# Spans of a gated linear attention: four short-format products on halves of the log decays in place of two f32 products

## The chip, the cores and the metric

The kernel runs on one core of one Trainium2 chip. The metric is the device time in microseconds (us) of one execution. A core has TensorE (PE, matrix products into PSUM), VectorE (DVE), ScalarE (ACT), GpSimd (POOL) and a queue for DMAs (SP). Each engine works through its own queue in order; between engines there are semaphores.

## The reference

One decoder layer on 1024 tokens of width 1024: a half-step SwiGLU network, a mixing layer of three head groups, a second half-step SwiGLU network. The change is in the mixing layer. Its linear-attention group takes this from the input projection:

```python
def gla(q, k, v, out_gate, gate_lr, w_gate_up, b_gate, norm_gain):
    log_a = jax.nn.log_sigmoid((gate_lr @ w_gate_up + b_gate).astype(jnp.float32)) / GLA_TAU
    ...
    b = jnp.cumsum(chunked(log_a, GLA_DK), axis=3)
    diff = b[..., :, None, :] - b[..., None, :, :]
    decay = jnp.exp(jnp.where(causal[:, :, None], diff, -jnp.inf))
    A = jnp.sum(qc[..., :, None, :] * kc[..., None, :, :] * decay, axis=-1)
    o_intra = jnp.einsum('bhnij,bhnjd->bhnid', A, vc)
    ...
    o_inter = jnp.einsum('bhncd,bhnde->bhnce', qc * jnp.exp(b), s_prev)
```

The sums of `log_a` over stretches of tokens are what the kernel calls spans. The other two groups are a sliding-window attention (window 128, 8 heads, with sinks and a relative bias) and an attention over 256 memory tokens (4 heads).

## The kernel before

The mix goes over the 1024 tokens in NB = 8 blocks of 128. The order on each engine is written out by hand, and semaphores with counts tie the engines together. I call one turn of the loop a pass; pass n does the work of block n and prepares block n + 1.

PE in pass n (`mix_tensor`): `mem_scores(n)` (L1809), `levels(n)` (L1841, 56 records), `turn(0, n)` (L1856, transposes of the probabilities of head group 0), `scores(0, n+1)` (L1753), `spans_of(n+1)` (L1763), `turn(1, n)` (L1856), the turned keys (L1863), `gla_out(n)` (L1879, L1882), `scores(1, n+1)`, `key_values(n)`, `turn(2, n)`, `values(0, n)` and `values(1, n)` (L1893), `mem_values(n)` (L1908). In pass 0 the memory scores and the levels stand slightly otherwise: the spans of block 0 and the scores of block 0 are made between the last products of the input projection, and `turn(0, 0)` is ahead of `levels(0)`.

`spans_of` multiplies the log decays of one block, `log_a[:, n, :]` (128x128, f32), by a constant matrix `spans` of zeros and ones (128x1024), in two products of 512 columns, into PSUM banks 2 and 3. An f32 product leaves two records in the trace. Products in the short format (F32R) leave one, and the kernel takes an f32 product elsewhere by splitting an operand in a high and a low half of that format (`split_product`, L57 to L59).

Three waits matter. `turn(1, n)` waits for `level_taken` at 7(n + 1): seven predicated copies on DVE (`take_levels`, L2088) which fetch the levels from the banks that the turn overwrites. `scores(0, n+1)` waits for the exponentials of memory attention of the same pass on ACT (`mem_exps`, L1986), which read the same banks. `spans_of(n+1)` waits for ACT's copy of the turned probabilities (`pt_copy(0, n)`, L2004), banks 2 and 3 again.

ACT in pass n (`mix_scalar`): the rest of `exps(1, n)` (L1969, L1974), `mem_exps(n)`, `pt_copy(0, n)`, `gate_decays(n+1)` (L1955 to L1962, the exponentials of the spans), `k_hat_copy` (L2009), `pt_copy(1, n)`, `o_copy`, `exps(0, n+1)`, `pt_copy(2, n)` (L1999), `swa_hi` (L2026), the first head of `exps(1, n+1)`, `mem_hi(n)` (L2031). In passes 4 and 5 a square (L1393) comes in before `mem_hi`.

DVE in pass n (`mix_vector`): `gate_edges` (L1793), `denominators(1, n)` (L1799, L1802), `take_levels(n)`, `mem_denominators(n)` (L2074; in pass 0 it is ahead of the copies), the row maxima of block n + 1 (L1773 to L1786), `gate_q` (L1823), `denominators(0, n+1)`, `swa_lo` (L2109), `mem_lo` (L2114), `mem_max(n+1)` (L1817). POOL scales the probabilities (L2172), four instructions for each head group, and makes two products (L2156, L2163).

SBUF places are given by address. The 4 KB from 84 KB on belong to `hT_lo[:, 5, :]`, which the input projection reads to its last product; that product signals `proj_ready` at NG.

Of the kernel before, what the change touches and what calls it, by code (L numbers as in the profile page):

```python
# [9 lines left out]
F32 = mybir.dt.float32  # L10
# [51 lines left out]
def build(nc, x_in, mem_in, w_gate1, w_up1, w_down1, w_proj, w_mem, w_out, w_gate2, w_up2, w_down2, gains_in,  # L62
# [3 lines left out]
    with ctx:  # L66
# [28 lines left out]
        def place(at, *tensors):  # L95

            skip = [(f"skip{next(places)}", [P, at // 4], F32)] if at else []
            return phase(*skip, *tensors)[len(skip):]
# [18 lines left out]
        for f, order in enumerate((PARTS, PARTS[4::-1] + PARTS[5:])):  # L117
# [36 lines left out]
        p_hi, p_lo = place(120 * KB, ("p_hi", [P, 3, D], F32R), ("p_lo", [P, 3, D], F32R))  # L154
        w_rank = place(176 * KB, ("w_rank", [P, KT, RANK_ROWS], F32))[0]
        p_raw = place(184 * KB, ("p_raw", [P, 3, D], F32))[0]
        (PT1, spans, Pg1, A_T0, A_T1, decays, edges, k_hat_tok, state, span_end, chunk_decay, row_max, shift, sink_shift,
         sink_exp, row_sum, row_inv) = place(
            120 * KB,
            ("PT1", [P, 2, HALF], F32), ("spans", [P, SPLITS + 1, P], F32), ("Pg1", [P, 4, 2 * P], F32),  # L160
            ("A_T0", [P, GLA_HEADS, P], F32), ("A_T1", [P, GLA_HEADS, P], F32),
            ("decays", [P, SPLITS + 2, P], F32), ("edges", [P, 2, 2, P], F32), ("k_hat_tok", [P, P], F32),
            ("state", [P, GLA_DV], F32), ("span_end", [P, NB], F32), ("chunk_decay", [P, NB], F32),
            ("row_max", [P, 8], F32), ("shift", [P, 12], F32), ("sink_shift", [P, 8], F32),
            ("sink_exp", [P, 8], F32), ("row_sum", [P, 12], F32), ("row_inv", [P, 12], F32))
        A_T = (A_T0, A_T1)
        square_hi = place(180 * KB, ("square_hi", [P, 2, HALF], F32R))[0]
        square_lo = place(196 * KB, ("square_lo", [P, 2, HALF], F32R))[0]
        bias, Pg0 = place(184 * KB, ("bias", [P, SWA_HEADS, 2 * P], F32), ("Pg0", [P, 4, 2 * P], F32))
# [1587 lines left out]
        def spans_of(pe, n):  # L1757
            wait(pe, pt_ready, pt_count(0, n - 1))
            if n == 0:
                pe.wait_ge(spans_landed, 16)  # L1760
                pe.wait_ge(gate_summed, 2)
            for c in range(2):
                mm = nc.tensor.matmul(ps[:, SPAN_BANK + c, :], log_a[:, n, :], spans[:, 4 * c:4 * c + 4, :],  # L1763
                                      start=True, stop=True)
            mm.then_inc(span_summed, 1)

        def bias_max(dve, u, n, heads=range(4)):
            dve.wait_ge(scored, unit_count(u, n))
# [20 lines left out]
        def gate_edges(dve, n):  # L1789
            dve.wait_ge(decay_ready, 4 * n + 4)  # L1790
            wait(dve, o_ready, n - 1)
            wait(dve, k_hat_turned, n - 1)
            nc.vector.tensor_tensor(edges[:, n % 2, :, :], decays[:, SPLITS:SPLITS + 2, :], gqk[:, :, blk(n)], ALU.mult  # L1793
                                    ).then_inc(edge_ready, 1)
# [152 lines left out]
        def mix_scalar(act):  # L1947
# [17 lines left out]
            def exps(u, n, heads=range(4)):  # L1965
                act.wait_ge(shifted, SHIFTS * n + 2 * u + 1)
                for i in heads:
                    p, c = P_of[u][:, i, band(n)], 4 * u + i
                    nc.scalar.activation(p, p, ACT.Exp, bias=shift[:, c:c + 1], accum_out=row_sum[:, c:c + 1]  # L1969
                                         ).then_inc(probs_ready, 1)  # L1970
                if 3 not in heads:
                    return
                act.wait_ge(shifted, SHIFTS * n + 2 * u + 2)
                nc.scalar.activation(sink_exp[:, 4 * u:4 * u + 4], sink_shift[:, 4 * u:4 * u + 4], ACT.Exp  # L1974
                                     ).then_inc(probs_ready, 1)
# [53 lines left out]
            def mem_hi(n):  # L2029
                act.wait_ge(values_done, values_count(2, n))  # L2030
                nc.scalar.activation(hT_hi[:, 6:8, blk(n)], ps[:, O_BANK, 2 * P:4 * P].rearrange("p (j t) -> p j t", j=2),  # L2031
                                     ACT.Copy).then_inc(mem_y_hi_ready, 1)
# [2 lines left out]
            nc.scalar.activation(rstd_tok[:, 0:1], eps[:], ACT.Exp)  # L2035
            gate_decays(0)
            exps(0, 0)
            for n in range(NB):
                more = n + 1 < NB
                exps(1, n, range(begun(n), 4))  # L2040
                mem_exps(n)
                if not more:
                    out_gate(n)
                pt_copy(0, n)
                if more:
                    gate_decays(n + 1)
                    k_hat_copy(n)
                else:
                    for c in range(2):
                        head_root(act, GLA_OUT + c, HALF)  # L2050
                pt_copy(1, n)
                if not more:
                    unit_scalar(act, NPROJ)
                o_copy(n)
                if more:
                    exps(0, n + 1)
                    if n:
                        out_gate(n)
                pt_copy(2, n)
                if n == 0:  # L2060
                    out_gate(n)
                swa_hi(n)
                if n in FIRST_SQUARE_AT:
                    first_square(FIRST_SQUARE_AT.index(n))
                if more:
                    exps(1, n + 1, range(begun(n + 1)))
                mem_hi(n)

        def mix_vector(dve):

# [41 lines left out]
            def mem_lo(n):  # L2112
                dve.wait_ge(mem_y_hi_ready, n + 1)
                nc.vector.tensor_tensor(hT_lo[:, 6:8, blk(n)],  # L2114
                                        ps[:, O_BANK, 2 * P:4 * P].rearrange("p (j t) -> p j t", j=2),
                                        hT_hi[:, 6:8, blk(n)].bitcast(F32), ALU.subtract).then_inc(mem_y_lo_ready, 1)

            for n in range(NB):
                more = n + 1 < NB
                if n:  # L2120
                    gate_edges(dve, n)
                if not more:
                    gate_out(n - 1)
                denominators(dve, 1, n)
                if n == 0:
                    mem_denominators(n)
                take_levels(n)
                if more:
                    if n:
                        mem_denominators(n)  # L2130
                    bias_max(dve, 0, n + 1)
                    bias_max(dve, 1, n + 1, (0, 1))
                    update_state(n)
                    sink_difference(dve, 0)
                    bias_max(dve, 1, n + 1, (2, 3))
                    sink_difference(dve, 1)
                    gate_q(dve, n + 1)
                    if n:
                        gate_out(n - 1)
                else:  # L2140
                    gate_out(n)
                    head_invert(dve, GLA_OUT, HALF)
                    unit_vector(dve, NPROJ)
                    gla_apply(dve, 0)
                if more:
                    denominators(dve, 0, n + 1)
                swa_lo(n)
                mem_lo(n)
                if more:
                    mem_max(dve, n + 1)  # L2150

# [210 lines left out]
        def _(sp):  # L2362
# [19 lines left out]
            skewed = bias_dram.rearrange("(h x) -> h x", h=SWA_HEADS)[:, P - 1:P - 1 + P * (ROW - 1)]  # L2382
            sp.dma_start(bias[:], skewed.rearrange("h (p u) -> p h u", u=ROW - 1)[:, :, 0:2 * P]).then_inc(bias_landed, 16)
            sp.wait_ge(proj_ready, last_group[PROJ.index("mq1")])
            sp.dma_start(spans[:], spans_dram).then_inc(spans_landed, 16)
            sp.wait_ge(biased, 8 * NB)
            unit_sync(sp, NPROJ)
            sp.wait_ge(turned, unit_count(0, NB - 1))
# [269 lines left out]
```

## Time and profile before

| what | value |
|---|---|
| device time, median of 3 runs | 1685.02 us (1684.78 to 1685.14) |
| device time of the profiled execution | 1685.07 us |
| its span | 1683.3 us |
| busy PE, DVE, ACT, POOL | 99%, 66%, 43%, 33% |
| spans product in the chain of work that ended last | 1% of the span |
| mixing passes 0 to 7 | about 840 to 950 us from the start |

The page's first part has the busy time of each engine. Its fourth follows the work that ended last back from the end. The timeline lists instructions with start and duration in us; in square brackets stands the idle time of that engine before the instruction and who ended it. Neighbouring instructions of one kind are merged in it (x7 is seven); a narrow slice shows single ones.

### The profile page before, as it was taken

To read this page: it belongs to the slowest core of one execution; us is meant where nothing else is said; L and a number is where in the kernel's file an instruction comes from. 1 tells how busy PE (TensorE), PEld (TensorE's weight loads), DVE (VectorE), ACT (ScalarE), POOL (GpSimd) and SP (SyncE) were. 2 spreads that over 40 slices of the span, in tenths; PEclk is the share of its full clock that TensorE was granted. 3 is DMA by queue.
4 is the path that set the end of the run, shared out by engine and by line. 5 is a ranking of instruction groups with operands and counts; after the bars stand their busy time and mean duration, and the time that the engine had idled before them with its cause. 6 is when DMAs were issued, how large, how long until landed. Compare 5 with 4: busy or idle time off the path is not lost.

```text
span 1683.3 us, 25076 instructions
## 1 busy us (share of the span) xinstructions
PE 1673.6 (99%) x8399; PEld 1373.2 (82%) x8399; DVE 1115.0 (66%) x1581; ACT 726.9 (43%) x1378; POOL 552.0 (33%) x457
## 2 busy tenths in 40 slices
PE   9999999999999999999999999999999999999999
PEld 7888888888888889888767787888888888888887
DVE  7965555555489588458888935985555555569664
ACT  6533333333344465333378723443333333334442
POOL 0544445544130135012266422354444444310000
PEclk9999999999999999999999999999999999999999
DMA  7342222233774532120100223123333222584434
GB/s 215 81 144 94 100 100 93 100 106 117 263 258 144 163 94 88 63 84 17 38 2 2 64 75 138 38 107 107 119 113 110 93 93 106 185 285 149 144 99 165
DMA packets 101790, 191.73 MB, mean 114 GB/s; under 512 B 11539, under 2 KB 14068, under 8 KB 101708
## 3 DMA queue, kind: packets, MB, share of 16 engines
q1 hardware_dynamic: 100624, 188.50, 32.9%
q0 software_dynamic: 848, 2.10, 1.0%
q8 instruction: 48, 0.79, 0.2%
q14 instruction: 34, 0.28, 0.0%
q10 hardware_dynamic: 236, 0.06, 0.0%
HBM read 139.76 MB, written 50.86 MB: 113 GB/s over the span
## 4 chain that ended last, share of the span: by engine, by line
PE 96%; ACT 1%; DVE 1%; DMA 1%; issue 0%; SPq 0%; ACTq 0%; DVEq 0%
PE ps L57 30%; PE ps L59 30%; PE ps L58 30%; PE ps L1856 1%; PE ps L1763 1%; PE ps L1893 1%; PE ps L1753 1%; PE ps L1841 1%; DMA xT<-in_x 1%; ACT Pg L1969 0%; PE ps L1908 0%; DVE A_T L2088 0%; PE ps L1809 0%; PE ps L1879 0%; ACT glu L2004 0%
## 5 line engine op out<-in xcount | busy, mean ns | idle before, releaser
L521 DVE TENSOR_TENSOR ring<-w_raw,ring 128x512 fp32r<-128x512 f32 x240 | 239.9, 1015 | 219.4 <-ACT ring L516 219.2
L57 PE MATMUL ps<-hiT,ring 128*128 128x512 f32 x672 | 261.6, 389 | 0.0
L59 PE MATMUL ps<-hiT,ring 128*128 128x512 f32 x672 | 261.5, 389 | 0.0
L58 PE MATMUL ps<-loT,ring 128*128 128x512 f32 x640 | 249.0, 389 | 0.0
L57 PE MATMUL ps<-down_ring 128*128 128x512 f32 x616 | 239.7, 389 | 0.0
L59 PE MATMUL ps<-down_ring 128*128 128x512 f32 x616 | 239.7, 389 | 0.0
L58 PE MATMUL ps<-down_ring 128*128 128x512 f32 x616 | 239.7, 389 | 0.0
L57 PE MATMUL ps<-hiB,ring 128*128 128x512 f32 x576 | 224.8, 390 | 0.3 <-DVE loB L386 0.3
L59 PE MATMUL ps<-hiB,ring 128*128 128x512 f32 x576 | 224.2, 389 | 0.0
L516 ACT ACTIVATE ring<-w_raw 128x512 fp32r<-128x512 f32 x240 | 150.5, 628 | 169.9 <-PE ps L59 163.4
L895 ACT ACTIVATE down_ring<-down_raw 128x512 fp32r<-128x512 f32 x176 | 108.9, 629 | 222.9 <-DMA down_raw<-act_dram 176.1
L899 DVE TENSOR_TENSOR down_ring<-down_raw,down_ring 128x512 fp32r<-128x512 f32 x176 | 128.2, 737 | 110.8 <-ACT down_ring L895 110.5
L537 POOL TENSOR_TENSOR w_raw<-w_raw 128x512 f32<-128x512 f32 x40 | 58.3, 1462 | 298.0 <-DVE ring L521 281.5
L58 PE MATMUL ps<-loB,ring 128*128 128x512 f32 x384 | 149.4, 389 | 0.0
L57 PEld LDWEIGHTS ps<-hiT,ring 128*128 128x128 f32 x672 | 126.2, 188 | 26.5 <-issue 0.3
L59 PEld LDWEIGHTS ps<-hiT,ring 128*128 128x128 f32 x672 | 126.2, 188 | 26.3
L58 PEld LDWEIGHTS ps<-loT,ring 128*128 128x128 f32 x640 | 120.1, 188 | 24.8
L58 PEld LDWEIGHTS ps<-down_ring 128*128 128x128 f32 x616 | 115.6, 188 | 24.2
L57 PEld LDWEIGHTS ps<-down_ring 128*128 128x128 f32 x616 | 115.7, 188 | 23.9
L59 PEld LDWEIGHTS ps<-down_ring 128*128 128x128 f32 x616 | 115.6, 188 | 23.9
L57 PEld LDWEIGHTS ps<-hiB,ring 128*128 128x128 f32 x576 | 108.1, 188 | 23.2 <-issue 0.9
L59 PEld LDWEIGHTS ps<-hiB,ring 128*128 128x128 f32 x576 | 108.1, 188 | 22.6
(296 smaller groups left out, 3004.8 us busy)
## 6 DMA issues: line engine op xcount, KB each, us to landing
down_raw<-act_dram SPq DMA_DIRECT2D x154, 256.0 KB, 2.6
w_raw<-in_w_gate SPq DMA_DIRECT2D x88, 256.0 KB, 3.1
w_raw<-in_w_up SPq DMA_DIRECT2D x88, 256.0 KB, 3.2
act_dram<-actT SPq DMA_DIRECT2D x88, 256.0 KB, 2.0
act_dram<-act SPq DMA_DIRECT2D x66, 256.0 KB, 2.0
wd<-in_w_down SPq DMA_DIRECT2D x44, 256.0 KB, 4.8
wd_mirrored<-in_w_down SPq DMA_DIRECT2D x33, 256.0 KB, 4.4
p_raw<-in_w_proj SPq DMA_DIRECT2D x15, 512.0 KB, 3.6
```

The lines of the kernel that those rows point to most:

```text
L57: nc.tensor.matmul(out, w_hi, x_hi, start=first, stop=False, skip_group_check=resumed)
L58: nc.tensor.matmul(out, w_hi, x_lo, start=False, stop=False, skip_group_check=resumed)
L59: return nc.tensor.matmul(out, w_lo, x_hi, start=False, stop=last, skip_group_check=resumed)
L516: nc.scalar.activation(ring[:, e % RING, 0, :], op_source(e), ACT.Copy).then_inc(op_hi, 1)
L521: nc.vector.tensor_tensor(ring[:, e % RING, 1, :], op_source(e), ring[:, e % RING, 0, :].bitcast(F32), ALU.subtract).then_inc(op_ready, 1)
L537: nc.gpsimd.tensor_tensor(w_of(x, "11"), w_of(x, "11"), w_of(x, "21"), ALU.subtract).then_inc(w_summed, 1)
L895: nc.scalar.activation(down_ring[:, down_slot(k), 0, :], down_source(f, k), ACT.Copy).then_inc(op_hi, 1)
L899: nc.vector.tensor_tensor(down_ring[:, down_slot(k), 1, :], down_source(f, k), down_ring[:, down_slot(k), 0, :].bitcast(F32), ALU.subtract ...
L1753: mm = nc.tensor.matmul(ps[:, score_bank(u, n) + g, at], qT[r, 2 * u + jj, blk(n)], kT[r, keys], start=True, stop=True)
L1763: mm = nc.tensor.matmul(ps[:, SPAN_BANK + c, :], log_a[:, n, :], spans[:, 4 * c:4 * c + 4, :], start=True, stop=True)
L1841: mm = nc.tensor.matmul(to, kg_of(n)[r, l, :], upper(qg_of(n)[r, l, :], l), start=True, stop=True)
L1856: tr = nc.tensor.transpose(ps[:, turn_bank(u, n) + kt, i * P:(i + 1) * P], probs_of(u, n)[:, i, kt * P:(kt + 1) * P], ident[:, :])
```

## The change

The spans of blocks 1 to 7 are made from two halves of `log_a`: `log_halves[:, 0, :]` is its rounding to the short format, made by ACT (`log_high`), and `log_halves[:, 1, :]` the difference, made by DVE (`log_low`). Each half is multiplied by the constant matrix in the short format, so there are four products in place of two; block 0 stays as it was. `log_halves` lies at 87 KB, so the first `log_high` waits for `proj_ready` at NG. The halves of block n + 2 are made at the end of pass n on both engines; those of block 1 at the start of the mix, on ACT ahead of the second head group's exponentials, on DVE ahead of `denominators(1, 0)`. `gate_summed` counts them: 2 for the log decays before, then one each.

```diff
+        spans = spans_r[:].bitcast(F32)
+        log_halves = place(87 * KB, ("log_halves", [P, 2, P], F32R))[0]
...
             if n == 0:
                 pe.wait_ge(spans_landed, 16)
                 pe.wait_ge(gate_summed, 2)
+            else:
+                pe.wait_ge(gate_summed, log_half_count(n, 1))
             for c in range(2):
-                mm = nc.tensor.matmul(ps[:, SPAN_BANK + c, :], log_a[:, n, :], spans[:, 4 * c:4 * c + 4, :],
-                                      start=True, stop=True)
+                of = slice(4 * c, 4 * c + 4)
+                if n == 0:
+                    mm = nc.tensor.matmul(ps[:, SPAN_BANK + c, :], log_a[:, n, :], spans[:, of, :], start=True, stop=True)
+                else:
+                    nc.tensor.matmul(ps[:, SPAN_BANK + c, :], log_halves[:, 0, :], spans_r[:, of, :], start=True, stop=False)
+                    mm = nc.tensor.matmul(ps[:, SPAN_BANK + c, :], log_halves[:, 1, :], spans_r[:, of, :], start=False,
+                                          stop=True)
             mm.then_inc(span_summed, 1)
+
+        def log_half_count(n, low):
+
+            return 2 * n + low + 1
+
+        def log_high(eng, n):
+            eng.wait_ge(proj_ready, NG)
+            wait(eng, span_summed, n if n > 1 else 0)
+            eng.activation(log_halves[:, 0, :], log_a[:, n, :], ACT.Copy).then_inc(gate_summed, 1)
+
+        def log_low(eng, n):
+            eng.wait_ge(gate_summed, log_half_count(n, 0))
+            eng.tensor_tensor(log_halves[:, 1, :], log_a[:, n, :], log_halves[:, 0, :].bitcast(F32), ALU.subtract
+                              ).then_inc(gate_summed, 1)
...
             exps(0, 0)
+            log_high(nc.scalar, 1)
             for n in range(NB):
...
                 mem_hi(n)
+                if n + 2 < NB:
+                    log_high(nc.scalar, n + 2)
...
                 if n:
                     gate_edges(dve, n)
+                else:
+                    log_low(nc.vector, 1)
...
                 mem_lo(n)
+                if n + 2 < NB:
+                    log_low(nc.vector, n + 2)
                 if more:
                     mem_max(dve, n + 1)
```

The queue of ACT at the start of the mix, before. `Pg` are the scores and probabilities of the window attention, `lo_raw` holds those of memory attention in pass 0, `glu` their turned copy.

```order
L1962 ACTIVATE decays<-ps,span_end 128x128
L1969 ACTIVATE Pg,row_sum<-Pg,shift 128x128 x4
L1974 ACTIVATE sink_exp<-sink_shift 128x4
L1969 ACTIVATE Pg,row_sum<-Pg,shift 128x128 x4
L1974 ACTIVATE sink_exp<-sink_shift 128x4
L1986 ACTIVATE lo_raw,row_sum<-ps,shift 128x256 x4
L2004 ACTIVATE glu<-ps 128x512
```

The same after.

```order
L1985 ACTIVATE decays<-ps,span_end 128x128
L1992 ACTIVATE Pg,row_sum<-Pg,shift 128x128 x4
L1997 ACTIVATE sink_exp<-sink_shift 128x4
L1783 ACTIVATE log_halves<-log_a 128x128
L1992 ACTIVATE Pg,row_sum<-Pg,shift 128x128 x4
L1997 ACTIVATE sink_exp<-sink_shift 128x4
L2009 ACTIVATE lo_raw,row_sum<-ps,shift 128x256 x4
L2027 ACTIVATE glu<-ps 128x512
```

The high half of block 1 has come between the exponentials of the two head groups; eight more exponential rows and the turned copy stand behind it.

The queue of DVE from the end of pass 0 into pass 1, before.

```order
L1799 TENSOR_TENSOR row_sum<-row_sum,sink_exp 128x4
L1802 RECIPROCAL row_inv<-row_sum 128x4
L2109 TENSOR_TENSOR hT_lo<-ps,hT_hi 128x4x128
L2114 TENSOR_TENSOR hT_lo<-ps,hT_hi 128x2x128
L1817 TENSOR_REDUCE shift<-ps 128x2 x2
L1793 TENSOR_TENSOR edges<-decays,gqk 128x256
L1799 TENSOR_TENSOR row_sum<-row_sum,sink_exp 128x4
L1802 RECIPROCAL row_inv<-row_sum 128x4
L2088 COPY_PREDICATED A_T<-masks,ps 128x4x64
```

The same after.

```order
L1822 TENSOR_TENSOR row_sum<-row_sum,sink_exp 128x4
L1825 RECIPROCAL row_inv<-row_sum 128x4
L2135 TENSOR_TENSOR hT_lo<-ps,hT_hi 128x4x128
L2140 TENSOR_TENSOR hT_lo<-ps,hT_hi 128x2x128
L1787 TENSOR_TENSOR log_halves<-log_a,log_halves 128x128
L1840 TENSOR_REDUCE shift<-ps 128x2 x2
L1816 TENSOR_TENSOR edges<-decays,gqk 128x256
L1822 TENSOR_TENSOR row_sum<-row_sum,sink_exp 128x4
L1825 RECIPROCAL row_inv<-row_sum 128x4
L2114 COPY_PREDICATED A_T<-masks,ps 128x4x64
```

The low half of block 2 has come between the memory subtraction and the row maxima of memory attention, with the seven predicated copies behind them.

The queue of PE in pass 1, after; before, one row `L1763 MATMUL ps<-spans,log_a 128x512 x2` stands for the four of L1771 and L1772.

```order
L1879 MATMUL ps<-ident,Pg 128x128 x8
L1755 MATMUL ps<-kT,qT 128x256 x4
L1771 MATMUL ps<-spans,log_halves 128x512
L1772 MATMUL ps<-spans,log_halves 128x512
L1771 MATMUL ps<-spans,log_halves 128x512
L1772 MATMUL ps<-spans,log_halves 128x512
L1879 MATMUL ps<-ident,Pg 128x128 x8
```

Nothing else moves on PE: turn(0), scores, spans, turn(1), as before.

## Rows read from the trace of the kernel before

**Rows 1.** The page: busy time of each engine in us, its share of the span.

```profile
PE 1673.6 (99%) x8399; PEld 1373.2 (82%) x8399; DVE 1115.0 (66%) x1581; ACT 726.9 (43%) x1378; POOL 552.0 (33%) x457
```

**Rows 2.** Chain of waits in pass 2: start us, us, engine and line.

```profile
872.98 1.98 PE ps L1763 x4
```

**Rows 3.** Timeline (start us, us, engine, line) in narrow slices: passes 2, 0, 6.

```profile
873.94 0.59 PE L1763 MATMUL ps<-spans,log_a 128*128 128x512 f32 x1
...
874.37 0.59 PE L1763 MATMUL ps<-spans,log_a 128*128 128x512 f32 x1
...
874.05 0.73 DVE L2088 COPY_PREDICATED A_T<-masks,ps 128x256 f32<-128x256 uint8 x1
...
874.93 0.41 PE L1856 MATMUL ps<-ident,Pg 128*128 128x128 f32 x2
...
845.81 0.72 DVE L2088 COPY_PREDICATED A_T<-masks,ps 128x256 f32<-128x256 uint8 x1
...
846.68 0.63 PE L1856 MATMUL ps<-ident,Pg 128*128 128x128 f32 x4 [1.08 <-DVE A_T L2088]
...
932.72 0.73 DVE L2088 COPY_PREDICATED A_T<-masks,ps 128x256 f32<-128x256 uint8 x1
...
933.82 0.27 PE L1856 MATMUL ps<-ident,Pg 128*128 128x128 f32 x1
```

**Rows 4.** Timeline of PE in the input projection, short-format products.

```profile
829.21 0.39 PE L59 MATMUL ps<-hT_hi,p_lo 128*128 128x512 f32 x1
829.44 0.39 PE L57 MATMUL ps<-hT_hi,p_hi 128*128 128x512 f32 x1
```

**Rows 5.** Timeline of ACT, POOL and DVE at the start of pass 0; a 128x128 copy.

```profile
837.09 0.39 ACT L1969 ACTIVATE Pg<-Pg,shift 128x128 f32<-128x128 f32 x1
...
840.43 0.20 ACT L1986 ACTIVATION_READ_ACCUMULATOR lo_raw<-ps,shift 128x1 f32 x1
...
840.11 0.15 POOL L2186 MEMSET state<- 128x64 f32 x1 [0.93 <-PE ps L59]
...
842.69 3.84 DVE L2088 COPY_PREDICATED A_T<-masks,ps 128x256 f32<-128x256 uint8 x7 [1.14 <-PE ps L1841]
...
847.45 0.28 ACT L2009 ACTIVATE k_hat_tok<-ps 128x128 f32<-128x128 f32 x1 [0.38 <-PE ps L1863]
```

**Rows 6.** Timeline of PE and ACT at the end of pass 0.

```profile
850.35 0.65 PE L1893 MATMUL ps<-glu,vg 128*64 128x256 f32 x4
...
851.10 0.60 ACT L1999 ACTIVATE glu<-ps 128x512 f32<-128x512 f32 x1
```

**Rows 7.** Timeline of DVE and POOL at the start of passes 2 and 1.

```profile
868.37 0.42 DVE L2114 TENSOR_TENSOR hT_lo<-ps,hT_hi 128x256 fp32r<-128x256 f32 x1
869.02 1.29 DVE L1817 TENSOR_REDUCE shift<-ps 128x2 f32<-128x512 f32 x2 [0.22 <-PE ps L1809]
870.22 0.42 DVE L1793 TENSOR_TENSOR edges<-decays,gqk 128x256 f32<-128x256 f32 x1
870.55 0.16 DVE L1799 TENSOR_TENSOR row_sum<-row_sum,sink_exp 128x4 f32<-128x4 f32 x1
...
867.65 1.84 POOL L2172 TENSOR_SCALAR Pg<-Pg,row_inv 128x256 f32<-128x256 f32 x4 [3.46 <-DVE row_inv L1802]
...
853.80 0.42 DVE L2114 TENSOR_TENSOR hT_lo<-ps,hT_hi 128x256 fp32r<-128x256 f32 x1
...
854.11 0.48 POOL L2172 TENSOR_SCALAR Pg<-Pg,row_inv 128x256 f32<-128x256 f32 x1
```

**Rows 8.** Timeline in pass 0: instructions of POOL and DVE side by side.

```profile
840.22 1.04 POOL L2156 TENSOR_TENSOR A_T<-ident,diag_of 128x512 f32<-128x512 f32 x1
...
840.70 0.58 DVE L1799 TENSOR_TENSOR row_sum<-row_sum,sink_exp 128x4 f32<-128x4 f32 x1
```

**Rows 9.** Timeline in pass 7: the same two engines side by side.

```profile
948.12 1.09 POOL L2172 TENSOR_SCALAR rstd<-rstd,row_inv 128x256 f32<-128x256 f32 x2
...
948.31 0.56 DVE L2104 SCALAR_TENSOR_TENSOR ggT<-qT,ggT 128x256 f32<-128x256 f32 x1
```

More of the change, by code:

```diff
@@ L156, in build @@
         p_raw = place(184 * KB, ("p_raw", [P, 3, D], F32))[0]
-        (PT1, spans, Pg1, A_T0, A_T1, decays, edges, k_hat_tok, state, span_end, chunk_decay, row_max, shift, sink_shift,
+        (PT1, spans_r, Pg1, A_T0, A_T1, decays, edges, k_hat_tok, state, span_end, chunk_decay, row_max, shift, sink_shift,
          sink_exp, row_sum, row_inv) = place(
             120 * KB,
-            ("PT1", [P, 2, HALF], F32), ("spans", [P, SPLITS + 1, P], F32), ("Pg1", [P, 4, 2 * P], F32),
+            ("PT1", [P, 2, HALF], F32), ("spans", [P, SPLITS + 1, P], F32R), ("Pg1", [P, 4, 2 * P], F32),
             ("A_T0", [P, GLA_HEADS, P], F32), ("A_T1", [P, GLA_HEADS, P], F32),
@@ L2384, in _ @@
             sp.wait_ge(proj_ready, last_group[PROJ.index("mq1")])
-            sp.dma_start(spans[:], spans_dram).then_inc(spans_landed, 16)
+            sp.dma_start(spans, spans_dram).then_inc(spans_landed, 16)
             sp.wait_ge(biased, 8 * NB)
```

## The prediction

> **What bounds the kernel now.** I read first the page's busy times: TensorE (PE) is busy 99% of the span and the next engine 66% [rows 1], so a microsecond taken from PE's own work looks like a microsecond gained. The change shortens PE's work in one line, the spans product, in blocks 1 to 7 of the mix. (I write spans(n) for the spans of block n; in the program's loop spans(n+1) is issued inside pass n, so passes 0 to 6 hold the short ones.) The chain of waits of pass 2 seems to confirm the gain: it books 1.98 us for the spans there [rows 2].
>
> The second view is the timeline around the end of the spans, in slices narrow enough to give single records, and it contradicts the chain. In pass 2 spans records follow each other by 0.43 us (873.94, 874.37), so PE was free at 874.80, yet turn(1) starts at 874.93. The last predicated copy of DVE, for whose `level_taken` turn(1) waits, ends at 874.05 + 0.73 = 874.78, which is 0.15 before. In pass 0, where the trace names that copy as the releaser, the distance is the same: 845.81 + 0.72 = 846.53, turn(1) at 846.68. So 0.15 is the time from copy to turn, and in pass 2 DVE's copies, not the spans, already set the start of turn(1), by 0.13 us. Passes 1, 3 and 4 repeat pass 2. In pass 6 ScalarE (ACT) makes the scores late; the copies end at 932.72 + 0.73 = 933.45 and would allow a turn at 933.60, and it starts at 933.82: there PE is last, by 0.22 [rows 3]. Two chains run side by side from the end of the level products: turn(0), scores, spans on PE, and seven copies on DVE. They are nearly equal, and the change shortens one.
>
> **The shorter spans.** A program product in f32 makes two records 0.43 us apart; two products make four, 1.72 us. Short-format products of the same 128x512 shape start 0.23 us apart in the projection (829.21, 829.44) [rows 4]. Four take 0.91 us, so PE is ready 0.8 to 0.9 us earlier. What is late next is the copies: passes 1 to 4 gain nothing, pass 5 I take at nothing, pass 6 gains at most 0.22. Pass 0 waits for the copy in any case. Bounds of this term: 0 and -0.22 by the rows, and -0.9 for each of six passes if the reading is wrong (a rival below).
>
> **The high half ahead of pass 0.** This is the large term. ACT's queue is in order, and the first `log_high` stands before the exponentials of pass 0 with a wait for `proj_ready` = NG, the last projection product. In the kernel before, ACT starts those exponentials at 837.09. GpSimd (POOL) has a wait for the same count, and its memset starts at 840.11, 0.93 us idle before it, released by PE. So ACT will stand for 840.11 - 837.09 = 3.02 us. The copy itself: a 128x128 copy on ACT (k_hat) is 0.28 long; I take 0.20 until the next can start, bounds 0.15 and 0.30. Behind it are eight exponentials with a small one, then four of memory attention, the last record of which ends at 840.43 + 0.20 = 840.63 without a wait in between. They now end at 840.63 + 3.02 + 0.20 = 843.85. DVE needs them for `mem_denominators(0)`, which stands before its copies; with 0.07 for the wait and 0.15 for that reciprocal the first copy starts at 844.07 instead of 842.69: 1.38 later [rows 5]. The seven copies take 3.84 as before and turn(1) moves by 1.38, from 846.68 to 848.06.
>
> PE has cover there: its scores also wait for the memory exponentials (same PSUM banks), start near 843.9, and with about 1.1 for them and 0.9 for the spans PE is ready at 845.9, well before 848.06. After turn(1) PE goes on in its order to the values; those of head group 0 end at 850.35 + 0.65 = 851.00, and ACT's next copy, which needs them, started at 851.10, held by ACT's own exponentials [rows 6]. With PE 1.38 later, PE becomes the releaser: 852.38, plus 0.07, 852.45 for 851.10. So 1.35 of the 1.38 arrives. Bounds 1.1 (ACT wakes faster, the chain behind has slack that I don't see) and 1.7 (log_high costs 0.3 and the wakes 0.1 each). Below zero is excluded here: the pass has nothing that becomes earlier on its last chain.
>
> **The halves at the end of passes 0 to 5.** On ACT `log_high` adds 0.2 us ahead of the remaining exponentials. These release the scores of the pass (by way of the PSUM banks), which then start up to 0.2 later; the 0.8 to 0.9 that the spans give back covers it, so I cost it at nothing. Without the shorter spans it would cost up to 0.2 a pass.
>
> On DVE `log_low` stands before `mem_max`, and everything from there to the copies is one unbroken queue of DVE work, so what it delays, turn(1) feels. In pass 2, at its start, DVE's memory subtraction starts at 868.37 (0.42), and mem_max at 869.02 after 0.22 us of idling for PE. The price: a 128x256 tensor_tensor in SBUF is 0.42, one of 4 columns 0.16, so 128 columns cost about 0.29, of which 0.13 is for the columns; the next starts 0.33 after the 0.42 one, so records overlap by 0.09 and the step is 0.20. Alone it would start at 868.70, let mem_max start at 868.90, and be free. But POOL runs four scales there, from 867.65 for 1.84 us [rows 7]. What two engines do to each other is seen in pass 0: a 4-column tensor_tensor on DVE with two SBUF inputs, 0.16 elsewhere, took 0.58 and ended at 841.28, beside a POOL tensor_tensor that ended at 841.26 [rows 8]. So log_low will wait for the running scale. Scales follow each other by 0.46; the third ends near 869.04, log_low ends 0.13 later, at 869.17, and mem_max can start at 869.08: 0.06 to 0.07 late. Passes 2 to 4: 3 x 0.07 = 0.21. In pass 1 DVE's subtraction starts at 853.80, so log_low would come at 854.13, just after the fourth scale (854.11, 0.48) [rows 7]: end 854.72, mem_max at 854.63 for 853.80 + 0.65 = 854.45: 0.18. Passes 5 and 6 have their 0.22 or so of room before DVE counts; I let log_low take 0.10 of pass 6's gain, which leaves -0.12. Bounds for the whole term: 0 (all in the idling), and 0.5 for each of six passes.
>
> The Trainium skill, page "SBUF — State Buffer", section "Who interferes with whom", speaks against this placement: a VectorE instruction with two SBUF inputs and a GpSimd instruction that reads SBUF exclude each other for a whole instruction. The 0.58 us instruction [rows 8] agrees. With this rule the sum is the one below; if no such blocking took place it would be 0.39 lower.
>
> **The sum.** 1.35 + 0.18 + 0.21 - 0.12 = +1.62 us. The profiled execution of before took 1685.07 us (span 1683.3), 0.05 over the median of its runs; after the mix PE is the bound again (its 99% in [rows 1]), so the delay passes to the end. 1685.07 + 1.62 = **1686.7 us**, a tenth of a per cent slower. I call 0.2%, or 3.4 us, what a measurement can tell from no change, so this is "the same". With the bounds 1.1 to 1.7 for the opening, and 0 to 1.2 for the rest, the likeliest case covers 1686.0 to 1687.9.
>
> **Rivals.**
> *A, PE really is last.* If the 0.13 us between 874.80 and 874.93 is only PE's change from one kind of product to another, the copies may end in time for an earlier turn. Then each of passes 1 to 6 gives back up to 0.9: 1685.07 - 5.4 + 1.35 + 0.4 = 1681.4. For it: the chain of waits [rows 2]. Against: the 0.15 us distance repeats to the hundredth where the copy is named as releaser, and in pass 6 it does not. Chance 5%.
> *B, log_low finds no gap between the scales.* If DVE gets its turn only after the fourth, it ends at 867.65 + 1.84 + 0.13 = 869.62 and mem_max starts 0.51 late, in passes 2 to 4; with 0.18 in pass 1 and 0.3 in each of 5 and 6 that is 2.3, and with the opening 3.65: 1688.7. It makes the kernel slower beyond 0.2% from a loss of about 0.4 a pass on. For it: the scales stand closely, one every 0.46 with records of 0.48 [rows 7]. Against: at 948.31 a DVE instruction with two SBUF inputs, 128x256, began during a scale and took 0.56, so 0.14 more than 0.42, while the two scales of POOL took 1.09, 0.17 more than two of 0.46 [rows 9]: it went in between. Chance 8%.
> *C, the stand at the opening is mostly absorbed,* because ACT's work can be caught up over the next pass or because the last projection ends earlier relative to ACT than I read: 1685.3 to 1685.8. For it: the opening is the one place where PE idles, so slack may hide there. Against: every step is a wait in the code. Chance 9%.
>
> **How the numbers follow.** Forecast 78%, A 5%, B 8%, C 9%. The range that holds it 8 times in 10 takes the forecast's bounds, and part of B and C: 1685.3 to 1688.3. Slower by over 0.2% (above 1688.4) is three quarters of B, 6%; faster is A, 5%; the rest, 89%, lies within 0.2%.
>
> **What would show it.** In the profile of the changed kernel: the four short spans records of a pass about 0.23 apart; ACT idle for about 3.0 us before its first log_halves row, released by PE; turn(1) of pass 0 about 1.4 later after the last projection product than before, and in passes 1 to 4 still 0.15 after the last predicated copy, with PE idle 0.8 us ahead of it; log_low rows of 0.4 to 0.5 us in place of 0.29; the steady period of a pass 0.07 longer. I am wrong if the period falls by some tenths (A), if log_low takes over 0.8 (B), if turn(1) of pass 0 moves by under 1 us (C), or if TensorE's granted clock falls in the longer idling of pass 0, which no row of before can show.

## The result, and the profile after

The changed kernel takes 1688.17 us (median of 17 runs, 1685.98 to 1689.14), the kernel before 1685.21 us in the same 17 rounds: ratio 1.0017, 95% interval 1.0010 to 1.0023. That is 3.0 us more, within the 0.2% that I had called the same, and inside the range forecast (1685.3 to 1688.3); but the time is 1.5 us over the forecast of 1686.7, and the difference of 3.0 us is 1.3 over the sum of 1.62. The reason was in none of my terms.

The page of the changed kernel (its profiled execution took 1687.79 us), busy time of each engine as in [rows 1]:

```profile
span 1686.0 us, 25103 instructions
...
PE 1670.1 (99%) x8399; PEld 1373.2 (81%) x8399; DVE 1115.8 (66%) x1588; ACT 729.2 (43%) x1385; POOL 549.8 (33%) x457
```

TensorE is busy for 3.5 us less and the span is 2.7 us longer. The timeline of pass 0 shows the opening; it answers to [rows 5]. First ACT at its stand, then the end of its exponentials, DVE's copies, and the rows of PE around its two idle stretches:

```profile
837.13 0.19 ACT L1997 ACTIVATE sink_exp<-sink_shift 128x4 f32<-128x4 f32 x1
...
840.22 0.31 ACT L1783 ACTIVATE log_halves<-log_a 128x128 fp32r<-128x128 f32 x1 [2.90 <-PE ps L59]
...
843.77 0.20 ACT L2009 ACTIVATION_READ_ACCUMULATOR lo_raw<-ps,shift 128x1 f32 x1
...
844.10 3.85 DVE L2114 COPY_PREDICATED A_T<-masks,ps 128x256 f32<-128x256 uint8 x7
...
844.03 1.14 PE L1755 MATMUL ps<-kT,qT 64*128 64x256 f32 x8 [1.27 <-ACT lo_raw L2009]
...
848.10 0.70 PE L1879 MATMUL ps<-ident,Pg 128*128 128x128 f32 x4 [1.81 <-DVE A_T L2114]
...
850.00 2.08 PE L1755 MATMUL ps<-kT,qT 64*128 64x256 f32 x8
```

Up to 848.10 this is the forecast: ACT idle for 2.90 us (forecast 3.0), exponentials done at 843.97 (843.85), copies from 844.10 (844.07), turn(1) at 848.10 (848.06). The last row is the surprise. Eight records of a scores product (first head group) took 1.14 us in the row of 844.03, and eight of the same shape (second head group) took 2.08 us six microseconds later. The view by stretches has the reason in its column PEclk, the clock that TensorE was granted (after PE and PEld come DVE, ACT and POOL, each busy us and number of instructions, then PEclk):

```profile
840.00:848.00 8.00, 4.67 (x73) 3.37 (x71) 5.66 (x14) 5.68 (x23) 5.89 (x12) 1.00 0.00 0
848.70:852.10 3.40, 3.40 (x25) 2.01 (x24) 0.90 (x5) 2.75 (x10) 0.89 (x1) 0.52 0.02 5
852.20:856.00 3.80, 2.98 (x38) 2.19 (x32) 3.38 (x15) 2.35 (x8) 0.25 (x1) 1.00 0.00 0
```

After a stretch of 8 us in which TensorE was busy for 4.67, it worked for 3.4 us at the lower of its two levels (0.52 in this stretch: 1.2 GHz, with a little of the upper level of 2.4 GHz at its end), and then at the upper one again. In the kernel before, TensorE is busy for 6.58 us in the same 8, and the granted clock is at the upper level through the whole mix.

The steady passes are told by pass 2, which answers to [rows 3] and [rows 7]:

```profile
871.84 0.47 DVE L1787 TENSOR_TENSOR log_halves<-log_a,log_halves 128x128 fp32r<-128x128 f32 x1
872.23 1.27 DVE L1840 TENSOR_REDUCE shift<-ps 128x2 f32<-128x512 f32 x2
...
873.95 0.18 DVE L1825 RECIPROCAL row_inv<-row_sum 128x4 f32<-128x4 f32 x1
874.04 0.91 DVE L2114 COPY_PREDICATED A_T<-masks,ps 128x256 f32<-128x256 uint8 x2
...
877.17 0.73 DVE L2114 COPY_PREDICATED A_T<-masks,ps 128x256 f32<-128x256 uint8 x1
...
876.16 0.50 PE L1771 MATMUL ps<-spans,log_halves 128*128 128x512 f32 x1
876.49 0.40 PE L1772 MATMUL ps<-spans,log_halves 128*128 128x512 f32 x1
876.73 0.40 PE L1771 MATMUL ps<-spans,log_halves 128*128 128x512 f32 x1
876.96 0.40 PE L1772 MATMUL ps<-spans,log_halves 128*128 128x512 f32 x1
878.04 0.63 PE L1879 MATMUL ps<-ident,Pg 128*128 128x128 f32 x4 [0.69 <-DVE A_T L2114]
```

From the second record on the spans are as short as forecast, 0.23 us a record (the first step is 0.33), and PE then idles for 0.69 us for DVE's last copy, which ends at 877.90; turn(1) follows 0.14 after it. The microsecond saved has turned into a wait.

Where the 2.7 us of span went, by the starts of rows in the two profiles (levels(n) is the first level product of pass n):

| stretch | before, us | after, us | difference | forecast |
|---|---|---|---|---|
| start to last projection product | 839.66 | 839.79 | +0.13 | 0 |
| last projection product to turn(1) of pass 0 | 7.02 | 8.31 | +1.29 | +1.38 |
| turn(1) of pass 0 to levels(1) | 7.80 | 9.39 | +1.59 | -0.03 |
| levels(1) to levels(2) | 14.57 | 14.69 | +0.12 | +0.18 |
| levels(2) to levels(5) | 43.83 | 43.82 | -0.01 | +0.21 |
| levels(5) to levels(7) | 29.63 | 29.26 | -0.37 | -0.12 |
| levels(7) to the end | 740.75 | 740.73 | -0.02 | 0 |

### The profile page after: what moved, and what is told of

Read it like the earlier page. It is cut to its first block, busy times and chain, and to the rows that moved or that the text cites. A ratio compares the mean times of both kernels' runs of the same rounds, so it can differ in the third digit from the quotient of the medians.

```text
span 1686.0 us, 25103 instructions
## 1 busy us (share of the span) xinstructions
PE 1670.1 (99%) x8399; PEld 1373.2 (81%) x8399; DVE 1115.8 (66%) x1588; ACT 729.2 (43%) x1385; POOL 549.8 (33%) x457
## 4 chain that ended last, share of the span: by engine, by line
PE 96%; DVE 2%; ACT 1%; DMA 0%; issue 0%; SPq 0%; ACTq 0%
PE ps L57 30%; PE ps L59 30%; PE ps L58 30%; DVE A_T L2114 2%; PE ps L1879 1%; PE ps L1916 1%; PE ps L1755 1%; PE ps L1864 1%; DMA xT<-in_x 0%; PE ps L1832 0%; PE ps L1931 0%; PE ps L1902 0%; PE ps L1413 0%; PE ps L1415 0%; PE ps L1458 0%
```

## The experiments

The theory after the result: 1.3 us from ACT's stand at the opening; some 1.6 us because TensorE, which idles in pass 0 for 1.27 and 1.81 us in place of one stretch of 1.08 (both kernels idle there for another 0.35 and 0.80), is granted the lower clock for a while after it; and a gain of 0.3 us from the later passes, where the copies hide the rest. The rival: the added work of the halves makes the difference, or is spread over the passes.

**Products of no use in the idle stretches.** The changed kernel with

```diff
+        FILL = (5, 4)
...
+            if n == 1:
+                for i in range(FILL[1]):
+                    nc.tensor.matmul(ps[:, SPAN_BANK, :], spans_r[:, 0, :], spans_r[:, 0:4, :], start=True, stop=True)
             for c in range(2):
...
                     levels(n)
+                    pe.wait_ge(decay_ready, 4)
+                    for i in range(FILL[0]):
+                        nc.tensor.matmul(ps[:, SPAN_BANK, :], spans_r[:, 0, :], spans_r[:, 0:4, :], start=True, stop=True)
```

that is, four ahead of the spans of block 1 and five behind `levels(0)`.

> The changed kernel with nine short-format products of no use (128x512, 0.23 us each) put into the two stretches of pass 0 in which TensorE idles: five after the level products, four ahead of the short spans products. Theory (clock): of the 3 us of the change, 1.6 come from the 3.4 us at the lower of TensorE's two clock levels that follow the idling of pass 0. With the idling filled the granted clock stays at its upper level and the time is about 1.6 us below the changed kernel: 1686.3, 1.1 over the kernel before; turn(1) of pass 0 stays where it is in the changed kernel, 1.3 later than before. Rival (work): the added time is that of log_high and log_low and of the stand of ScalarE alone; then the fillers change nothing and the time stays at 1688.2.

Measured: 1686.83 us (11 runs) against 1685.55 for the kernel before on that chip, ratio 1.0008 (0.9999 to 1.0017). More work on the busiest engine made the kernel 1.3 us faster than the changed one. In its profile turn(1) of pass 0 starts 8.32 us after the last projection product (8.31 in the changed kernel), so the stand is all there, and from turn(1) to levels(1) it takes 7.89 us in place of 9.39. Its granted clock in the same part of the program (PE alone in this answer: busy us, instructions, PEclk):

```profile
844.00:848.00 4.00, 4.00 (x21) 1.00 0.00 0
848.00:852.00 4.00, 3.12 (x33) 1.00 0.01 4
852.00:856.00 4.00, 3.09 (x33) 1.00 0.00 0
```

This is the clock's share, separated from the stand's. Ten of the eleven executions have a mean granted clock of 1.000, one (1688.00 us) has 0.999. The rival of added work falls: the halves are all still made.

**The halves of block 1 earlier, at another place.**

```diff
-            eng.wait_ge(proj_ready, NG)
+            eng.wait_ge(proj_ready, NG if n > 1 else NG - 1)
...
+        log_halves_first = place(80 * KB, ("log_halves_first", [P, 2, P], F32R))[0]
```

with `log_halves_first` in place of `log_halves` for block 1.

> The changed kernel, but the halves of block 1 lie at 80 KB, in the part of hT_lo that the last but one projection group frees, so that ScalarE's first log_high waits for proj_ready at NG - 1 and does not stand. The rest as in the changed kernel. Theory: ScalarE's stand of 2.9 us goes, the first predicated copy is back at 2.9 us after the last projection product, and turn(1) of pass 0 where it was before. What stays is -0.3 us from the last passes, so 1684.9 if the granted clock stays up. But TensorE now idles from the end of the shorter spans to turn(1) of pass 0, 1.9 us in place of 1.1; if that is enough for the lower clock level, 1.6 us come on top: 1686.5. Rival (the halves themselves cost): the time stays over 1687.

Measured: 1685.93 us (11 runs), before 1685.55; ratio 1.0003 (0.9994 to 1.0012). ACT does not stand: its log_high starts at 837.15 right behind the small exponential, and turn(1) of pass 0 comes 7.03 us after the last projection product.

```profile
837.05 0.19 ACT L2001 ACTIVATE sink_exp<-sink_shift 128x4 f32<-128x4 f32 x1
837.15 0.29 ACT L1787 ACTIVATE log_halves_first<-log_a 128x128 fp32r<-128x128 f32 x1
...
846.75 0.41 PE L1883 MATMUL ps<-ident,Pg 128*128 128x128 f32 x2 [1.87 <-DVE A_T L2118]
```

TensorE idles for 1.87 us once. The executions fall into two groups: six took 1684.8 to 1685.9 us at a mean granted clock of 1.000, five took 1686.9 to 1687.4 at 0.999. The profiled one (1685.15 us) is of the first: from turn(1) of pass 0 to levels(1) it takes 7.80 us, as in the kernel before. Whether the clock falls after these idle stretches is settled anew in each execution.

**The halves made, the spans as before.**

```diff
-                if n == 0:
+                if True:
                     mm = nc.tensor.matmul(ps[:, SPAN_BANK + c, :], log_a[:, n, :], spans[:, of, :], start=True, stop=True)
```

> The changed kernel with its halves made and waited for, but with all spans made by the two f32 products on log_a as before (the halves are not used). This is the change's cost without its saving. Theory: opening +1.3 as in the changed kernel; TensorE's second idling in pass 0 is 0.9 us shorter (about 0.9 in place of 1.8), so the granted clock stays up; the passes after it cost 0 to 0.2 each because TensorE is last again and ScalarE's 0.2 is no longer covered: 1686.5 to 1687.5, and the granted clock 1.0. Rival 1: the clock falls here too (the first idling of 1.3 us or the stand as a whole does it): 1688 to 1689. Rival 2 (the shorter spans do gain 0.9 a pass): this kernel is then slower than the changed one by 4 to 5 us: 1692.

Measured: 1688.40 us (11 runs), before 1685.55; ratio 1.0017 (1.0008 to 1.0026). I had the opening right and the clock wrong: it fell here too, so the first rival came true. Eight of the 11 executions have a mean granted clock of 0.998 or 0.999; the other three, given as 1.000, still took 1687.7 to 1688.4 us. In the profile it fell even sooner and for longer, around the end of the first idle stretch, of 1.27 us. The timeline of PE, where eight scores records take 2.08 us and the four f32 spans records 3.78:

```profile
844.27 2.08 PE L1755 MATMUL ps<-kT,qT 64*128 64x256 f32 x8 [1.27 <-ACT lo_raw L2009]
846.28 3.78 PE L1769 MATMUL ps<-spans,log_a 128*128 128x512 f32 x4
```

The view by stretches, PEclk in the third column from the right:

```profile
840.00:844.00 4.00, 2.65 (x62) 2.15 (x60) 2.12 (x5) 3.54 (x17) 2.24 (x6) 0.97 0.00 0
844.00:850.60 6.60, 6.33 (x16) 3.34 (x17) 5.35 (x17) 1.20 (x5) 3.14 (x6) 0.50 0.01 2
```

So the idling that the shorter spans add is not needed for the fall; the stand alone can bring it. The second rival falls as well: without the short products the ratio to the kernel before is 1.0017, the same as with them, and not 4 to 5 us more. The passes give the sizes: levels(2) to levels(5) takes 43.77 us, so making the halves costs nothing there; levels(5) to levels(7) takes 30.03 us for 29.63 before and 29.26 after. There ACT's 0.2 us for log_high is exposed once in each pass (turn(1) comes 6.29 us after the start of the levels in passes 5 and 6, for 6.09 before), and the short spans cover it (5.88).

**Products of no use in the second idle stretch only.** The first experiment without its first five products:

```diff
-        FILL = (5, 4)
+        FILL = (0, 4)
```

> The changed kernel with four products of no use in its second idle stretch of pass 0 only (1.8 us become 0.9); the first, 1.27 us ahead of the scores, stays. Theory: what counts is how long TensorE idles in the pass as a whole; with 2.2 us in place of 3.1 only part of the runs fall to the lower clock level, and the median lies between the filled kernel (1686.8) and the changed one (1688.2). Rival: the second stretch alone is the cause; then it reads as the filled kernel, 1686.8, in all runs. Third possibility: the first stretch alone is the cause, and the time stays at 1688.2.

Measured: 1687.82 us (11 runs), before 1685.54; ratio 1.0013 (1.0004 to 1.0022). It lies between the two, nearer to the changed kernel. In the profiled execution (1689.0 us) the clock was down at the time of the four fillers: they follow each other at about 0.47 us, and the idle stretch behind the spans is gone altogether.

```profile
845.62 1.68 PE L1756 MATMUL ps<-kT,qT 64*128 64x256 f32 x8 [1.36 <-ACT lo_raw L2016]
847.22 2.07 PE L1769 MATMUL ps<-spans 128*128 128x512 f32 x4
```

The same stretch in the view by stretches:

```profile
845.00:849.50 4.50, 3.88 (x13) 2.79 (x14) 3.79 (x9) 0.95 (x4) 3.40 (x7) 0.62 0.00 0
```

Six of the 11 executions have a mean clock of 0.999 (1687.3 to 1689.0 us), five of 1.000 (1686.9 to 1688.0): the remaining first stretch is enough in part of the runs. Those five, though, are by their median 0.9 us above the kernel with both stretches filled, which a mean clock of 1.000 does not explain and no run settles. How much each stretch adds to the chance can't be told from 11 runs each.

**Block 1's halves behind the exponentials of pass 0.**

```diff
             exps(0, 0)
-            log_high(nc.scalar, 1)
...
                 mem_exps(n)
+                if n == 0:
+                    log_high(nc.scalar, 1)
...
                 if n == 0:
                     mem_denominators(n)
+                    log_low(nc.vector, 1)
                 take_levels(n)
```

(and `log_low` is taken from its place ahead of `denominators(1, 0)`).

> The changed kernel with one thing moved: the halves of block 1 are made behind the exponentials of pass 0, not ahead of them (log_high after mem_exps(0) on ScalarE, log_low after mem_denominators(0) on VectorE). All memory places and waits stay. Theory: by then the last projection product is done and ScalarE does not stand: idle before its first log_high under 0.1 us in place of 2.9, turn(1) of pass 0 some 7.0 us after the last projection product in place of 8.3; 1.3 us of the change go in any case. TensorE idles 1.9 us once in pass 0, so the runs fall in two kinds as with the early halves: about half near 1685.1, half near 1687.1. Rival: if the place of the halves and not the order was to blame, it stays near 1688.

The changed kernel itself, on the same chip:

> The changed kernel itself once more, on the same chip as the two above, so that they can be compared directly. Theory: 1688.2, with most runs showing a stretch of lower clock; 3.0 above the reordered kernel's faster kind of run (1.3 the stand, 1.7 the clock).

Measured: 1685.76 us (1684.78 to 1687.97, 11 runs) for the reordered kernel and 1688.08 us (1686.72 to 1689.00, 11 runs) for the changed one, before 1685.38; ratios 1.0004 (0.9995 to 1.0013) and 1.0015 (1.0006 to 1.0024). At the same memory place another order takes the stand away, as another place did above. ACT's wait is over when it gets there:

```profile
840.25 0.20 ACT L2009 ACTIVATION_READ_ACCUMULATOR lo_raw<-ps,shift 128x1 f32 x1
840.35 0.31 ACT L1783 ACTIVATE log_halves<-log_a 128x128 fp32r<-128x128 f32 x1
...
846.51 0.30 PE L1879 MATMUL ps<-ident,Pg 128*128 128x128 f32 x1 [1.88 <-DVE A_T L2115]
```

Turn(1) of pass 0 is 7.04 us after the last projection product, as in the kernel before. Seven of its executions took 1684.8 to 1686.1, four 1687.1 to 1688.0, three of these at a mean clock of 0.999 and one (1687.12) at 1.000. The kernel before also took 1686.9 to 1687.1 in three of its 27 executions of this comparison, at 1.000: not every slower execution is a fall of the clock. All 11 executions of the changed kernel here are at 0.998 or 0.999. The second profile of the changed kernel shows the same fall as the first:

```profile
844.00:848.00 4.00, 2.20 (x15) 1.35 (x12) 3.79 (x10) 1.54 (x5) 3.42 (x6) 1.00 0.00 0
848.00:852.00 4.00, 4.00 (x30) 2.48 (x29) 1.55 (x8) 3.09 (x11) 1.23 (x1) 0.57 0.02 4
852.00:856.00 4.00, 3.20 (x34) 2.28 (x35) 3.56 (x16) 2.55 (x9) 0.69 (x2) 1.00 0.00 0
```

**No stand, and the idling filled.** The two kernels without a stand, each with four products of no use ahead of the spans of block 1 (and the wait for `decay_ready` behind `levels(0)`, as in the first experiment):

```diff
+        FILL = (0, 4)
...
+            if n == 1:
+                for i in range(FILL[1]):
+                    nc.tensor.matmul(ps[:, SPAN_BANK, :], spans_r[:, 0, :], spans_r[:, 0:4, :], start=True, stop=True)
```

> The kernel with the early halves of block 1 (at 80 KB, wait for NG - 1), and four short-format products of no use ahead of the short spans products of pass 0, which leaves about 0.95 us of idling there in place of 1.87. Theory (clock): the early kernel has two kinds of runs, about half at a mean granted clock of 1.0 and 1684.8 to 1685.9, half at 0.999 and 2 us longer. With the filler all runs are of the first kind: median 1685.2, that is 0.3 to 0.4 below the kernel before on the same chip. Rival: the second kind of run has another cause; then some 5 of 11 runs stay above 1686.8, and the median near 1686.

> The same, with four short-format products of no use ahead of the short spans products of pass 0. Theory: idling 0.95 us, granted clock up in all or nearly all runs, all of them between 1685.0 and 1686.3, median 1685.5: nothing gained or lost against the kernel before, since the 0.4 us that the last passes give are as large as the scatter. Rival: with every loss gone the shorter spans show as a gain of over 1 us: under 1684.5.

Measured: early with fillers 1685.94 us (11 runs), before 1685.54, ratio 1.0004 (0.9994 to 1.0013); behind with fillers 1686.27 us (11 runs), before 1685.38, ratio 1.0002 (0.9993 to 1.0011). PE idles for 0.98 us in both. The mean granted clock is 1.000 in all 22 executions, where 8 of the 22 without fillers had 0.999. By time the slower group is gone but for one execution (1688.13) among the early ones; the rest lie between 1684.9 and 1687.0. The medians, though, are 0.4 and 0.9 over the kernel before, not 0.3 below it or level with it. The mix itself is shorter in the profiles (levels(1) to levels(7) takes 87.69 and 87.77 us for 88.03), so the difference lies outside it or in scatter: in the second of them the last projection product starts at 841.38, 1.7 us later than in the kernel before, in a part of the program that no edit touches. I leave open where that comes from. No version that makes all of its levels is faster than the kernel before by more than the comparison can tell.

**Are the copies really what bounds the passes?** The last two of the seven predicated copies made for one head only (a part of the levels is left out), in the kernel before and in the kernel with early halves:

```diff
+                    if l >= 5:
+                        to, mask, got = to[:, 0:1], mask[:, 0:1], got[:, 0:1]
                     nc.vector.copy_predicated(to, mask, got).then_inc(level_taken, 1)
```

> The kernel before with the last two of the seven predicated copies of each pass made for one head only (64 of 256 columns): a part of the levels is left out. The copies then end about 1 us earlier. Theory: in passes 1 to 4 TensorE is only 0.13 us behind the copies, in pass 6 and 5 it is last already, so turn(1) comes forward by 0.13 in four passes; with up to 1 us in pass 0 and 7, together 1 to 2.5 us: 1683.0 to 1684.5. Rival (the spans are no bound at all): each pass gains the full 1 us of the copies: 1677.

> The kernel with early halves and short spans, with the same two light copies (a part of the levels is left out). Theory: with the copies out of the way the short spans give what the change could have given: turn(1) follows the end of the spans, about 0.7 us earlier in each of passes 1 to 6 than in the kernel before with light copies, 4 to 5 us in all: 1679 to 1680 where the clock stays up. Rival: something else is as near as the copies were (ScalarE's copy of the turned probabilities, POOL's scales), and the gain over the light kernel before is under 1.5 us.

Measured: 1684.41 us (10 runs) and 1679.77 us (5 runs), before 1685.54; ratios 0.9994 (0.9984 to 1.0003) and 0.9965 (0.9952 to 0.9978). Pass 2 of the light kernel before, then of the light kernel with short spans:

```profile
873.77 0.30 DVE L2090 COPY_PREDICATED A_T<-masks,ps 128x64 f32<-128x64 uint8 x1
...
874.10 1.02 PE L1763 MATMUL ps<-spans,log_a 128*128 128x512 f32 x2
874.96 0.27 PE L1856 MATMUL ps<-ident,Pg 128*128 128x128 f32 x1
```

```profile
872.16 0.30 DVE L2120 COPY_PREDICATED A_T<-masks,ps 128x64 f32<-128x64 uint8 x1
...
872.35 0.40 PE L1776 MATMUL ps<-spans,log_halves 128*128 128x512 f32 x1
872.61 0.30 PE L1883 MATMUL ps<-ident,Pg 128*128 128x128 f32 x1
```

In the first the copies end 0.9 us before the turn, and turn(1) comes 5.75 us after levels(2) where it was 5.88: the 0.13 us that I had read in [rows 3], to the hundredth. Freed of the copies the f32 spans bind, and little is won: 1.1 us, not clear of the scatter. In the second the turn starts 0.26 us after the last short record, whose step is 0.23, and again 0.15 behind the last copy (872.46): even the light copies end last, by some 0.03. From levels(1) to levels(7) it takes 83.56 us for 87.47: the short products are worth 3.9 us in six passes once the copies are shorter, and 4.6 us in the whole kernel; most of the rest is in pass 0, where turn(1) to levels(1) takes 7.80 us for 8.55. The change speeds up the right engine in the wrong order: the copies would have to be shortened first.

## Why the prediction was right, and where it failed

**What bounds the kernel.** Right, and shown: the short spans gain nothing in passes 2 to 4 (43.83 and 43.82 us), turn(1) stays 0.14 to 0.15 behind the last copy, and the light kernels separate the two chains. Rival A is refuted, as is the chain of waits as a price list: it booked 1.98 us for the spans, and halving them moved nothing.

**The stand at the opening.** Right in mechanism and nearly in size: forecast 1.38 at turn(1), measured 1.29. ACT woke 0.1 sooner than I had set, at 2.90 us of idling. Rival C is refuted; the two kernels without the stand have it back.

**"PE has cover there".** This is the step that failed, though the time lay in the range. I wrote that PE would be ready at 845.9 and wait until 848.06, and costed this idling at nothing, since nothing waits for PE in it. In the profile it cost 1.59 us afterwards, through the granted clock: products at half the rate for 3.4 us. I named a fall of the clock only in my last sentence, as a sign of being wrong, without a price or a chance. Its price for each microsecond could have been written down (at half the clock a stretch costs half its length); that the stretch would be 3.4 us long is first seen in this profile. The Trainium skill, page "TensorE: Matmul & The Clock Gate", part 1, says that a clock gate in front of TensorE passes a share of the pulses that is set by how busy TensorE was of late. The traces agree, with 1.00 and 0.52 on either side of 848.7.

**What turn(1)'s delay leaves at the end of pass 0.** The 1.35 of 1.38 can't be seen in the changed kernel, where the clock lies over it; in the kernel with fillers the stretch from turn(1) to levels(1) is 0.09 longer than before, so the delay passes on.

**log_low beside the scales.** Half right. It was delayed as read: 0.58 us in pass 1, 0.47 in passes 2 to 4, 0.41 in 5 and 6, and 0.71 in pass 0 beside a product of POOL of 1.04 us, against the 0.29 that I had estimated for it alone (0.26 in the two kernels with the order changed, where it starts in pass 0 while POOL is idle). mem_max came 0.08 late against the levels (forecast 0.07) in pass 2. But the copies came only 0.02 late. "One unbroken queue" was wrong: the first copy starts 0.09 after the reciprocal's start in the changed kernel and 0.14 in the one before, where it still waited for the level products. That give of 0.05 or so took up the 0.07. Forecast 0.21 for passes 2 to 4, measured 0; pass 1, 0.18 and 0.12. Rival B is refuted: DVE did get in between the scales. The delay is not the same in every execution. In the second profile of the changed kernel the log_low of pass 1 took 0.29 us, the scale beside it 0.59 in place of 0.48, and levels(1) to levels(2) 14.58 us, 0.01 over the kernel before: there the scale was held up and the subtraction was not.

```profile
856.71 0.29 DVE L1787 TENSOR_TENSOR log_halves<-log_a,log_halves 128x128 fp32r<-128x128 f32 x1
...
856.68 0.59 POOL L2202 TENSOR_SCALAR Pg<-Pg,row_inv 128x256 f32<-128x256 f32 x1
```

The rule of the Trainium skill, page "SBUF — State Buffer", section "Who interferes with whom", is borne out by the seven durations of the first profile, all over 0.29, and by the two rows above; what I made of it in time was not.

**Passes 5 and 6.** Forecast -0.12, measured -0.37: pass 6 gained 0.18, where I had 0.12, and pass 5 gained 0.19, where I had nothing. In pass 5 the first copy stood 2.08 us behind the start of the levels in the kernel before and 2.07 in the light one; in all profiles with halves it is 1.85 to 1.88, also in the one whose spans are f32. So it comes sooner with the halves and not with the short spans. By what mechanism is not shown.

**The sum.** Forecast +1.62; measured without the clock +1.1 (2.7 less 1.6), with it +2.7 in the profile and +3.0 in the medians. The time lies above the 1687.9 of my likeliest case. The range held because its upper end had been stretched for rival B, a mechanism that wasn't there; that was luck. Two sums were also off: the bounds of the likeliest case give 1686.2 to 1688.0, and the 1.2 us in them for everything behind the opening is worked out nowhere; and without blocking the sum would have been 0.49 lower, not 0.39, since pass 6 too had 0.10 for log_low.

## What to carry to other kernels

A saving on the busiest engine is worth what the next chain to the same wait leaves: compare the end of the work with the end of the other thing waited for, record by record, before trusting the shares of a chain. Put a step whose inputs or place come free late behind the work that doesn't need it, in a queue that runs in order; here moving two calls took back 1.3 us and brought part of the executions back to the time of the kernel before. And idling of TensorE in an otherwise dense program is not free even where nobody waits for it: ask for how long it grows, and put half the length of a stretch at the lower clock (here 3.4 us, so 1.7) into the sum as a case of its own.

## What the runs showed of the hardware

The clock level after a short idling is not the same in every execution. With one idle stretch of 1.08 us in pass 0 the profile of the kernel before keeps the upper level. With 1.87 us, five executions of eleven were 2 us longer at a lower mean clock; with 1.88 us, three of eleven had the lower mean clock. With 1.27 and 1.81 us, 15 of 17 executions of the changed kernel had a mean clock of 0.998 or 0.999 (1687.7 to 1689.1 us) and two of 1.000 (1685.98 and 1688.11), and in the repeat all 11 were at 0.998 or 0.999. With the idling filled to 0.98 us all 22 executions were at 1.000. The stretch at the lower level was 3.4 us in two profiles of the changed kernel and over 6 us in the one with the halves alone.

A DVE subtraction of 128x128 with both inputs in SBUF took 0.26 us where it started with POOL idle, 0.41 to 0.58 us beside POOL's scales and 0.71 beside a longer product of POOL, depending on where in the POOL instruction it came. It got in between two scales that stood 0.46 us apart. Where it took 0.29 us, just behind the start of a scale, the scale took 0.59 in place of 0.48: either of the two can be the one that is held up.
